# One attention stage of a two-block model: copies ahead of exponentials on ScalarE, half of the probability scaling on GpSimd, the compressed branch two steps later

## What is computed

```python
def native_sparse_attention(q, kc, vc, ks, vs, kw, vw, gate_logits, ...):
    ...
        pc = jnp.where(mc, jax.nn.softmax(jnp.where(mc, sc, NEG_INF), axis=-1), 0.0)
        o_cmp = jnp.einsum('bghqn,bgne->bghqe', pc.astype(dt), v_cmp)
    ...
        ps = jax.nn.softmax(ss.reshape(B, C_KV_GROUPS, C_HPG, C_QBLOCK, -1), axis=-1).reshape(ss.shape)
        o_slc = jnp.einsum('bghqnk,bgqnke->bghqe', ps.astype(dt), vg)
    ...
        pw = jax.nn.softmax(jnp.where(mw, sw, NEG_INF), axis=-1)
        o_win = jnp.einsum('bghqk,bgke->bghqe', pw.astype(dt), vwi)
        return gi[..., 0:1] * o_cmp + gi[..., 1:2] * o_slc + gi[..., 2:3] * o_win

    h = num / jnp.maximum(jnp.abs(den), jnp.exp(-m_s))[..., None]
    h = rmsnorm(h, norm_w.reshape(D_HEADS, D_V)).reshape(B, T, D_OUT)
    return h.astype(og.dtype) * jax.nn.sigmoid(og)
```

## Time and profile before

| what | value |
| --- | --- |
| median of 3 runs | 2870.78 us |
| time of the profiled execution | 2868.78 us |
| its span, first to last instruction | 2867.0 us |
| mean granted clock of TensorE | 0.963 of full |
| TensorE busy over the span | 2704.0 us (94%) |
| VectorE busy | 1509.2 us (53%) |
| ScalarE busy | 986.6 us (34%) |
| GpSimd busy | 350.5 us (12%) |

### The profile page before, as it was taken

One profiled execution on the slowest core, in us unless ns is written; L12 is line 12 of the kernel. 1 busy time (PEld: TensorE's weight loads), 2 busy tenths in 40 slices (PEclk: granted clock), 3 DMA queues, 4 the chain that ended last, 5 costly groups with the idle time before them and its releaser, 6 DMA issues.

```text
span 2867.0 us, 32354 instructions
## 1 busy us (share of the span) xinstructions
PE 2704.0 (94%) x13312; PEld 2142.0 (75%) x13312; DVE 1509.2 (53%) x2062; ACT 986.6 (34%) x1662; POOL 350.5 (12%) x306
## 2 busy tenths in 40 slices
PE   7879998999999988899999999999999977999998
PEld 6767876788888665586788888888878534788886
DVE  7965897544334678546434334343365367543333
ACT  3214654422222533543322223222233335332221
POOL 0001001222200001000222102221000000122200
PEclk9979999999999998799999999999999878999999
DMA  3333112122232221001333332223322200133232
GB/s 137 76 83 127 62 53 70 65 98 99 97 96 93 74 67 47 8 2 61 102 99 100 96 98 94 96 96 100 98 92 96 68 15 1 52 104 100 98 94 83
DMA packets 77539, 229.04 MB, mean 80 GB/s; under 512 B 16976, under 2 KB 18256, under 8 KB 77136
## 3 DMA queue, kind: packets, MB, share of 16 engines
q1 hardware_dynamic: 64464, 213.51, 22.9%
q0 software_dynamic: 1840, 5.77, 1.1%
q10 hardware_dynamic: 11088, 7.70, 0.9%
HBM read 221.18 MB, written 5.77 MB: 79 GB/s over the span
## 4 chain that ended last, share of the span: by engine, by line
PE 79%; DVE 13%; ACT 5%; issue 1%; DMA 1%; ACTq 1%; POOL 0%; DVEq 0%; POOLq 0%
PE ps L354 78%; DVE mem L371 5%; DVE part L441 2%; ACT part L429 1%; PE ps L365 1%; DVE mem L384 1%; DMA mem<-lag_dram 1%; DVE mem L2887 1%; DVE mem L377 1%; DVE ps L371 1%; ACTq L1139 1%; DVE mem L389 1%; DVE mem L549 0%; ACT mem L505 0%; DVE mem L630 0%
## 5 line engine op out<-in xcount | busy, mean ns | idle before, releaser
L354 PE MATMUL ps<-part,part 128*128 128x512 f32 (+2 forms) x9918 | 2277.4, 391 | 41.3 <-DVE part L441 18.2
L354 PEld LDWEIGHTS ps<-part,part 128*128 128x128 f32 x9918 | 1855.1, 189 | 461.1 <-DVE part L441 22.0
L441 DVE TENSOR_TENSOR part<-mem,part 128x1024 fp32r<-128x1024 f32 (+2 forms) x421 | 561.2, 1340 | 579.6 <-ACT part L429 579.1
L429 ACT ACTIVATE part<-mem 128x1024 fp32r<-128x1024 f32 (+2 forms) x421 | 417.5, 1002 | 224.6 <-DMA mem<-in_ffb_down 56.7
L371 DVE TENSOR_TENSOR mem<-ps,mem 128x512 f32<-128x512 f32 (+2 forms) x296 | 195.6, 661 | 345.3 <-PE ps L354 335.7
L354 PE MATMUL ps<-mem 128*64 128x64 f32 (+13 forms) x2568 | 273.1, 317 | 60.3 <-DVE mem L371 29.3
L354 PEld LDWEIGHTS ps<-mem 128*64 128x64 f32 (+4 forms) x2568 | 185.3, 169 | 138.8 <-issue 54.5
L513 POOL TENSOR_TENSOR mem<-mem 128x512 f32<-128x512 f32 x62 | 80.8, 1304 | 1132.5 <-ACT mem L505 1131.5
L1557 ACT ACTIVATE part<-mem 128x512 fp32r<-128x512 f32 x88 | 55.6, 632 | 328.5 <-DVE mem L371 328.5
L371 DVE TENSOR_TENSOR mem<-mem 128x512 f32<-128x512 f32 (+10 forms) x289 | 141.8, 491 | 43.2 <-ACT mem L1584 11.4
L1554 ACT ACTIVATE mem<-mem 128x512 f32<-128x512 f32 x88 | 55.6, 632 | 314.2 <-DVE mem L371 314.2
(11 more groups left out here) (178 smaller groups left out, 1060.8 us busy)
## 6 DMA issues: line engine op xcount, KB each, us to landing
mem<-in_ffa_gate SPq DMA_DIRECT2D x44, 512.0 KB, 3.2
mem<-in_ffa_up SPq DMA_DIRECT2D x44, 512.0 KB, 3.2
mem<-in_ffb_gate SPq DMA_DIRECT2D x44, 512.0 KB, 3.2
mem<-in_ffb_up SPq DMA_DIRECT2D x44, 512.0 KB, 3.2
mem<-in_ffa_down SPq DMA_DIRECT2D x32, 512.0 KB, 3.5
mem<-in_ffb_down SPq DMA_DIRECT2D x32, 512.0 KB, 3.6
mem<-in_w_odd SPq DMA_DIRECT2D x24, 512.0 KB, 3.2
mem<-in_w_ab SPq DMA_DIRECT2D x22, 512.0 KB, 3.2
```

Of the source, the lines that this page charges most:

```text
L354: return e.matmul(out, l, r, start=start, stop=stop, skip_group_check=True)
L429: w.e.activation(K.wts[c % NH].h[:, 0:n], K.raws[c % NR][:, 0:n], ACT.Copy).then_inc(*K_A.up(("w", c)))
L441: w.e.tensor_tensor(t.l, K.raws[c % NR][:, 0:n], t.hf, SUB).then_inc(*K.V.up(("w", c)))
```

## The change

It has five parts, and all of them lie in the fourth mixer.

1. On ScalarE the copy of the transposed probabilities of step i - 2 moves from behind the exponentials of step i to the head of the step.
2. The scaling of the probabilities of group 1 moves from VectorE to GpSimd, as a product with a column broadcast along the row; VectorE keeps group 0. TensorE waits for both counts.
3. `first_of(q)` becomes 8q - 1 in place of 8q - 3, so the compressed branch of heads 1 to 3 runs two steps later on TensorE, VectorE and ScalarE. Head 0 stays at step 0.
4. The reciprocal of 4 x 512 numbers becomes two of 4 x 256, at steps 4 and 5 of VectorE.
5. The mask no longer waits for VectorE's own last instruction.

```diff
 def first_of(q):
-    return max(8 * q - 3, 0)
+    return max(8 * q - 1, 0)
...
             for g in range(2):
                 acc = K.take(w, ("npt", u, g), K.A, bank=4 + g)
-                w.wait_ge(*K.V["npr", u, g])
+                w.wait_ge(*(K.V, K.G)[g]["npr", u, g])
...
         w.wait_ge(*K.A["root"])
-        recip(w, a, a, "factors")
+        half = a[:, 256 * (part - 2):256 * (part - 1)]
+        w.e.reciprocal(half, half).then_inc(*K.V.up("factors"))
...
             w.wait_ge(*K.P["nscore", i])
-            tt(w, both[:, :, t * P:n], both[:, :, t * P:n], b(K.cc("negmask"), [P, 2, P], 1), ADD)
+            w.e.tensor_tensor(both[:, :, t * P:n], both[:, :, t * P:n], b(K.cc("negmask"), [P, 2, P], 1), ADD).then_inc(
+                *K.V.up())
...
-            tt(w, st[:, 4:6], st[:, 4:6], E.gates(t, hd, 1 + br), MUL)
-            for g in range(2):
-                pr = E.pr[u % 3][:, g, 0:n]
-                ts(w, pr, pr, st[:, 4 + g:5 + g], None, MUL, None, ("npr", u, g))
+            tt(w, st[:, 4:6], st[:, 4:6], E.gates(t, hd, 1 + br), MUL, ("nfactor", u))
+            pr = E.pr[u % 3][:, 0, 0:n]
+            ts(w, pr, pr, st[:, 4:5], None, MUL, None, ("npr", u, 0))
...
-        if i in (1, 2, 4):
-            mlstm_rows_vector(K, w, (1, 2, 4).index(i))
+        if i in (1, 2, 4, 5):
+            mlstm_rows_vector(K, w, (1, 2, 4, 5).index(i))
...
     for i in range(34):
+        if i >= 2:
+            u = i - 2
+            n = (STEPS[u][2] + 1) * P
+            w.wait_ge(*K.P["npt", u])
+            if u > 1:
+                w.wait_ge(*K.P["npv", u - 2])
+            e.activation(E.pt[u % 2][:, :, 0:n], K.ps[:, 4:6, 0:n], ACT.Copy).then_inc(
+                *K.A.up(("npt", u, 0), ("npt", u, 1)))
         if i < 32:
...
     memset(w, E.kcd, 0.0, "vcm_zeros")
+    for u in range(32):
+        n = (STEPS[u][2] + 1) * P
+        pr = E.pr[u % 3][:, 1, 0:n]
+        w.wait_ge(*K.V["nfactor", u])
+        w.e.tensor_tensor(pr, pr, E.st[u % 4][:, 5:6].to_broadcast([P, n]), MUL).then_inc(*K.G.up(("npr", u, 1)))
```

More of the change, by code:

```diff
@@ L3084, in nsa_scalar @@
                 e.activation(E.ptc[q % 2][0:64, :], K.acc("cpt", q)[0:64, :], ACT.Copy).then_inc(*K.A.up(("cpt", q)))
[L3085 to L3092, removed]
         if i == 3:
```

## The result

| what | before | after |
| --- | --- | --- |
| median of 15 runs each | 2872.54 us | 2865.89 us |
| ratio, 95% interval | | 0.9975 (0.9966 to 0.9983) |
| profiled execution, its span | 2868.78, 2867.0 us | 2865.16, 2863.3 us |
| mean granted clock | 0.963 | 0.963 |

The change is faster by 6.6 us, some 0.25%. The forecast was 17 us less, with a range that ended at 2864; the sign is right, and the size is less than half of it.

The account below looks back on a forecast made before the run. It took TensorE's 35.2 idle us in the fourth mixer's loop, 19.5 of them waiting for the copy, as the bound. Copy order and split 11, less 0.5, plus 1, 2, 1 and clock 2, rounded to 17, gave 2853.8 us, range 2846 to 2864.

Parts of the forecast that it names:

- The frame: Fourth mixer's loop: a microsecond saved there reaches the program's end whole, and nothing outside the loop changes.
- The copy's wait: TensorE's 19.5 us wait before transposes falls under 8; copy order and scaling split together save 11 us, bounds 4.7 to 19.5.
- The two steps that I costed: Loop steps 25 and 27 at full clock: order and split win 2.2 of 3.7 us of waiting.
- The ports: At each scaling VectorE takes the shared SBUF ports first and GpSimd starts when it ends; 0.5 us counted for collisions elsewhere.
- The rival with the ports: GpSimd gets the ports first and VectorE's scaling waits, costing 12.6 us: 7.9 slower, 2878.7 us; chance 0.04.
- The cover: Transposes of group 0 hide GpSimd's later group 1, with 0.72 us slack at 512 columns; no cost counted, up to 12.6.
- The first rival: TensorE waits for GpSimd's late half in wide steps, taking back some 8 us: 2861.8 us; chance 0.14.
- The small parts: Gains in the loop: compressed branch later 2 us, reciprocal in halves 1, mask without its own wait 1.
- the sum: Loop gains added: 11 - 0.5 + 1 + 2 + 1 + 2 = 16.5, rounded to 17 us.
- The clock: Less TensorE idling raises the loop's granted clock above 0.82, saving 2 us, bounds -4 to 11.
- my second estimate: From the loop's chain: half the scaling, 5.9 us, plus exponentials ahead of a copy, 4.7, together 10.6 us.

Follow-up runs that it names:

- e1: The kernel before with only the copy moved ahead of the exponentials on ScalarE: 2859.91 us, ratio 0.9960.
- e3: The changed kernel with both groups scaled on VectorE again, all other parts kept: 2860.14 us, ratio 0.9954 to the kernel before.
- e4: The changed kernel with GpSimd waiting for VectorE's scaling of group 0 instead of the factor: 2854.94 us, ratio 0.9939 to the kernel before.
- e2: The kernel before with only group 1's scaling moved to GpSimd: 2873.27 us, ratio 1.0004.
- e6: The changed kernel with both scalings on VectorE, plus a GpSimd product on a spare tile that TensorE waits for: 2872.91 us, ratio 1.0001 to the kernel before.
- e11: The changed kernel with GpSimd clearing one unused column between factor and product, delaying the product some 0.2 us: 2847.59 us, ratio 0.9919 to the kernel before.
- e9: The kernel before with only the compressed branch two steps later: 2867.91 us, ratio 0.9986.
- e7: The changed kernel with GpSimd waiting for VectorE's scaling and the compressed branch back at 8q - 3: 2854.41 us, ratio 0.9931 to the kernel before.
- e5: The changed kernel with group 1 scaled on ScalarE, behind the next step's exponentials, instead of GpSimd: 2857.80 us, ratio 0.9947 to the kernel before.

## Why the prediction was right in sign and wrong in size

**The frame** held. What the loop saves reaches the end of the program: 6.56 us in the loop, 6.65 in the medians. That the two agree so closely is partly chance, since the rest of the program took between 2726.1 and 2732.5 us in the 13 profiles, though none of its code changed.

**The copy's wait** held: 19.5 us became 0.5, under the 8 foretold. But its size was set too low. In e1 the order alone gave 11.5 us, as much as I had counted for order and scaling together, and over twice the 4.7 that I had set as its lower bound. The two steps that I costed could have told me. With the order alone and both scalings left on VectorE, the transposes would start at about 2422.60 instead of 2423.55, and at about 2428.49 instead of 2429.57. That is 2.0 us of the 2.2 that I gave to both parts together. The 4.7 us, the exponentials' share of the chain, was no bound for the order.

**The ports: this step failed.** "So VectorE is first, and GpSimd starts when it ends; this is how I summed above." The rows were read rightly: VectorE does start 0.04 us after the factor and GpSimd a little later. What failed is the next thought, that the one whose start is recorded first has the ports and GpSimd then waits for the scaling's end. VectorE has the earlier record in the steps of the changed kernel and lost in all 32; GpSimd's product starts 0.02 to 0.05 us behind the scaling's start, and VectorE is the one that waits. So VectorE's scalings, which were to shrink from 24.7 us in sum to 12.4, grew to 30.2, and the split, counted as a gain, cost some 6 us of time (e3); with VectorE kept first it gains some 5 (e4). "I am wrong on the ports if L377's mean for 512 columns exceeds 0.49 us": it is 1.363. The loop ended at 2444.84 and not near 2431.5.

The Trainium skill, SBUF — State Buffer, section "SBUF: two separate sides", says of GpSimd and a VectorE instruction in a two-port mode that whichever of the two starts first gets the pair for the whole instruction, and the other fully blocks. That one of them is held, the traces of the changed kernel, e2 and e6 show (1.363 us in place of 0.487 in the first). By the starts in the record, "first" does not hold at a lead of 0.05 us, and does at 0.20 (e11), and "fully" is true but for some 0.15 us. The size can be read closely. In the changed kernel VectorE's instruction is longer than alone by the product's own time less 0.16 us, at all four widths:

| columns | VectorE after, alone, difference | GpSimd's product | product less difference |
| --- | --- | --- | --- |
| 512 | 1.363, 0.487, 0.876 | 1.039 | 0.163 |
| 384 | 1.085, 0.420, 0.665 | 0.826 | 0.161 |
| 256 | 0.804, 0.353, 0.451 | 0.612 | 0.161 |
| 128 | 0.525, 0.287, 0.238 | 0.399 | 0.161 |

(alone by the groups of e3.) The sum of the differences over 8 steps each is 8 x 2.23 = 17.8 us, and e6 found 18.1. The same is seen in the earlier trace rows: there VectorE's instruction (a subtraction of two tiles, which the prediction calls a product) lasts 2.25 - 1.22 = 1.03 us more than alone, 0.14 less than the 1.17 that GpSimd still had to go. And e11's product, which starts with 0.29 us of the scaling to go, grows by 0.14.

**The rival with the ports** was the true mechanism, at a chance of 0.04, and still not the true outcome: it put the time at 2878.7. Its price was over twice too high, 12.6 us where VectorE's scalings grew by 5.5 in sum. With the products' true times its formula gives 9.4, for they are quicker than I estimated (1.04, 0.83, 0.61, 0.40 us for my 1.29, 0.98, 0.66, 0.34; they multiply by one column that is read again and again, where the earlier trace rows have two full tiles). The other 3.9 are 32 times the 0.12 us by which VectorE stands for less than I took. Besides the price, the order was set at 4.7 us there and measured at 11.5. With the measured terms it would have read: order and small parts together 11.3 us (e3, by the medians; 13.2 by its ratio), less 5.7 for the ports (VectorE's busy time), so 5.6 to 7.5 faster; the result is 6.6. This adds up terms that were measured afterwards and is no forecast.

**The cover.** The wait for GpSimd's late half came to nothing in the changed kernel, as no transposes are put down to L3123. It couldn't show there, since VectorE's held scaling ends after the product (2421.54 against 2421.26 in the step above). In e4, where the product comes last, they wait 2.1 us for it. The first rival is wrong as a mechanism, though the time (2861.8) is nearer to the result than the forecast was.

**The small parts.** Part 3 gave 3.6 us alone, where I took 2: the wait for the bank (4.9 us) is gone. Part 4 gave 3.4, where I took 1 and had 1.7 as the bound; the interval (0.3 to 5.5 us) does not exclude 1.7. Together with the mask they gave 6.2. But beside the order they add little: e3 (order and small parts) has 2860.14 and e1 (order alone) 2859.91, and by the ratios e3 is ahead by 1.7 us. Here a second step failed, **the sum**: 11 + 1 + 2 + 1 were added as if each wait were its own. Were they, e3 would be 17.7 us faster than the kernel before (11.5 + 6.2), which is the very end of its interval (17.8); it was 11.3. TensorE's idle time says the same: the order takes 7.6 us off it, the small parts 6.5, both together 10.9. My reading is that they partly remove the same idle time, as e9's longer wait for the copy and e7 suggest for part 3; which of the waits it is for each part was not followed further.

**The clock** stayed where it was, 0.81 to 0.82; TensorE's busy time fell by 2.1 us. That is the 2 us that I had, but by luck: the term was meant for 15 us less idling, and only 4.5 came; in e4, where 14.7 came, the busy time fell by 1.2. The range of 93.7 to 108.4 us over the experiments says that this term was worth a wider range than most of the mechanisms.

The forecast as a whole, 2853.8 us, is what the change does when VectorE is first: 2854.94 in e4. There the split brings 5.2 us (2860.14 of e3 less 2854.94, though the two intervals overlap), near the 5.9 of my second estimate. But the agreement of the whole is luck: the order and the split together bring 16.7 us where I had 11, and the small parts next to nothing where I had 4, so the errors cancel.

## What to carry to other kernels

When work on SBUF data is split between VectorE and GpSimd, don't let both start on one event: look whether the instruction that stays on VectorE has grown, since the time it stands is recorded inside it and not as idle time. If it has, let GpSimd wait for VectorE's instruction, or start some 0.2 us behind it; here that was worth more than the change itself. And where several parts of a change work on the same idle time, their gains may not add, as with the order and the small parts here: cost each one on a timeline in which the others are already made.

## What the runs showed of the hardware that was not expected

- Beside a product of GpSimd, a recorded lead of 0.02 to 0.05 us does not save VectorE's scaling from being held (32 of 32 steps, changed kernel); a lead of 0.18 to 0.25 us does (scaling of 512 columns at 0.486 us, e11). Where between them it turns was not tried.
- The loser's instruction grows by the winner's remaining recorded time less 0.14 to 0.16 us: VectorE's in the changed kernel and in the earlier trace rows, GpSimd's in e11.
- GpSimd's clearing of one column, which reads nothing, starts 0.03 us behind VectorE's scaling in e11, doesn't lengthen it (0.486 us), and isn't held by it either (0.10 us).
- A product with one column broadcast takes GpSimd 1.04 us for 512 columns, a product of two full tiles 1.29.
- ScalarE's scaling of 512 columns took 0.72 us (e5). Where it overlapped VectorE's most, for 0.25 us in one step, VectorE's stayed at 0.48 us.
